# Layer 0's activations normalised before the projection, and ScalarE instead of VectorE evicting its tiles

## Chip, cores and metric

One core of a Trainium2 chip runs one inference step. The metric is the device time of that core in microseconds, the median of several executions; lower is better.

## What is computed

A decoder of two layers works on 512 prompt rows and 8 sample rows of width 1024. Layer 0 is a Mamba-2 state-space mixer, layer 1 a gated position mixer; each is followed by a squared-ReLU MLP. The part that matters here, from the reference:

```python
def rmsnorm(x, g):
    xf = x.astype(jnp.float32)
    r = lax.rsqrt(jnp.mean(xf * xf, axis=-1, keepdims=True) + RMS_EPS)
    return (xf * r * g.astype(jnp.float32)).astype(x.dtype)
...
    proj = h @ w_in                       # h = rmsnorm(x): 1024 -> z, x/B/C, dt
    ...
    conv = conv_b + xbc_ext[:, 0:l] * conv_w[0]
    for k in range(1, SSD_CONV_K):
        conv = conv + xbc_ext[:, k:k + l] * conv_w[k]
    xbc_act = jax.nn.silu(conv)
    ...
    dt = jax.nn.softplus(dt_raw + dt_bias)
    y, h_final = ssd_scan(xs, dt, A, Bm, Cm, h0)
    y = (y + xs * d_skip) * jax.nn.silu(z)
```

## The kernel before

All activations lie transposed, features on the 128 partitions and the 520 rows along the free axis (`xT`, 8 tiles). Every product is done in three passes for accuracy: weights and activations are split into a high and a low part (`w_hi`, `w_lo`, `h_hi`, `h_lo`), so a **unit** of 128 output features is 8 tiles x 3 products x 2 halves of some 260 rows, 48 matmuls (L500), into two PSUM banks. Units come in **pairs** of 256 weight columns. A pair is loaded by SyncE, its high part is written by ScalarE (`split_w`, L897), its low part by VectorE (L1492), each when the pair before last has been multiplied. Two slots of banks (0, 1 and 2, 3) alternate, so a unit waits until the unit before last has been evicted.

The RMS norm of x is not applied to x but to the results: x is only multiplied by the gain, the projection is computed from that, and each evicted tile is multiplied by `rstd`, one value per row, repeated on all partitions. That needs the squares of `xT` (ScalarE, L916), their sum over tiles (GpSimd, L1342), the sum over partitions by a matmul (`stats`, L543), a root (ScalarE, L929) and a reciprocal of 520 values (VectorE, L1515).

Layer 0 does first the pair of dt (32 columns, padded to 128), then for each of 8 groups six units: C and B (0, 1), the two x tiles (2, 3) and two z tiles (4, 5). A **window** `g` on each engine is the work of group g's scan together with units 4 and 5 of g and units 0 to 3 of the next group; every engine has this order written out by hand. The out-projection stands in two parts, after windows 4 and 7. VectorE's part of a window is its queue of:

- `evac_unit`: raw convolution tile out of PSUM times `rstd` (L1561 for the samples' columns, L1563 for the prompt's), or z times `rstd` (L1498), which ScalarE then puts through silu in place (`silu_z`, L1003);
- `conv`: the taps 1 to 3 (L1575), after ScalarE has written tap 0 (`tap0`, L992) from the evicted tile;
- `decayed` (L1606), `y_norm` (L1584, L1587), `sample` (product L1618, reduction L1622), the multiply by decay `xdte` (L1724), `states` and `combine` (ends with L1675).

GpSimd's part is a sum of squares (`y_sum`, L1356), loading of the sample states, two at a time, and four times per window their update: decay L1410, outer product L1420, addition L1424 twice each; then the stores, and once per window two low parts (L1366). It begins, beside the sum, with a small transfer (L1400) of B and C, which ScalarE evicts (L1106). `sample` n on VectorE waits for update n on GpSimd, the sum waits for two squares by ScalarE (L1024), and these wait for `combine`. TensorE's small transposes of the raw tiles (`raw_tr`, L583) wait for their eviction.

At the start SyncE loads x in four chunks of 128 rows, ScalarE issues some 17 small transfers, and TensorE transposes x (L554) and the convolution's parameters (L568). After the dt unit a chain of small operations on ScalarE and VectorE gives the decays (L1144 to L1157, L1749 to L1765), TensorE transposes them (L720) and VectorE copies them (L1768).

## Time and profile before

| | |
|---|---|
| median of 3 executions | 1663.0 us (1662.29 to 1666.39) |
| span of the profiled execution | 1663.9 us |
| TensorE busy | 1560.4 us, 94% |
| VectorE busy | 942.6 us, 57% |
| ScalarE busy | 593.2 us, 36% |
| GpSimd busy | 389.1 us, 23% |
| granted TensorE clock, mean | 0.976 |
| HBM over the span | 103 GB/s |

The span runs from the first to the last instruction of the core. The profile gives no other time for that execution: its span lies 0.9 us above the median, and what lies around it is within the spread of the executions. In 40 slices of the span TensorE is at nine tenths or more from the 17th on; its gaps are in the first 600 us.

### The profile page before, as it was taken

The numbers are of one execution on the slowest core, as the hardware profiler recorded it, in microseconds if no ns is written. First come the engines' busy times: TensorE is split into PE (matmuls) and PEld (weight loads), VectorE is DVE, ScalarE is ACT, GpSimd is POOL, SyncE is SP. The second block draws the span as 40 slices with busy tenths as digits, with TensorE's granted clock in tenths as the row PEclk, the third lists the DMA queues.
The fourth block names the chain that finished last, engine by engine and source line by source line (L and its number), as shares of the span: only waits on it lengthen the run. The fifth ranks groups of instructions, "written<-read, shape, count | busy, mean of one in ns | idle before, by whom it ended". The sixth has DMA issues, their size and how long they took to land.

```text
span 1663.9 us, 30150 instructions
## 1 busy us (share of the span) xinstructions
PE 1560.4 (94%) x12617; PEld 1538.8 (92%) x12617; DVE 942.6 (57%) x1101; ACT 593.2 (36%) x755; POOL 389.1 (23%) x437
## 2 busy tenths in 40 slices
PE   5898988899887999999999999999999999999996
PEld 5888888899887899999999999999999999999996
DVE  4688898863988774343435453464445435344353
ACT  3746644625465342221212343432234212122221
POOL 3076676631777420000000122100001000000001
PEclk9999999899998999999999999999999999999998
DMA  5445354433444323233232333222232332323221
GB/s 162 110 138 155 122 159 144 133 125 112 132 151 131 118 77 102 76 102 98 79 101 77 102 102 102 77 79 77 80 99 77 102 100 79 103 77 102 77 77 52
DMA packets 158919, 173.34 MB, mean 104 GB/s; under 512 B 13912, under 2 KB 146896, under 8 KB 158784
## 3 DMA queue, kind: packets, MB, share of 16 engines
q1 hardware_dynamic: 137032, 131.30, 25.8%
q0 software_dynamic: 9472, 26.50, 4.9%
q10 hardware_dynamic: 12288, 13.71, 2.9%
q8 instruction: 97, 1.59, 0.4%
q14 instruction: 30, 0.25, 0.0%
HBM read 159.53 MB, written 12.21 MB: 103 GB/s over the span
## 4 chain that ended last, share of the span: by engine, by line
PE 64%; DVE 1%; ACT 1%; issue 0%; POOL 0%; ACTq 0%; DVEq 0%
PE ps L500 61%; PE ps L842 1%; PE ps L520 0%; PE ps L810 0%; ACT w_hi L897 0%; PE ps L757 0%; DVE h_lo L1509 0%; PE ps L543 0%; DVE xT L1805 0%; DVE w_lo L1492 0%; POOL ssum L1356 0%; ACT arena L1300 0%; PE ps L834 0%; POOL arena L1424 0%; DVE work L1498 0%
## 5 line engine op out<-in xcount | busy, mean ns | idle before, releaser
L500 PE MATMUL ps<-h_hi,w_hi 128*128 128x260 f32 (+2 forms) x2320 | 485.5, 291 | 12.2 <-issue 4.9
L500 PE MATMUL ps<-h_lo,w_hi 128*128 128x260 f32 (+2 forms) x2320 | 474.9, 287 | 0.1
L500 PE MATMUL ps<-h_hi,w_lo 128*128 128x260 f32 (+2 forms) x2320 | 474.8, 287 | 0.0
L1492 DVE TENSOR_TENSOR w_lo<-w,w_hi 128x2048 fp32r<-128x2048 f32 (+2 forms) x122 | 278.7, 2285 | 185.6 <-ACT w_hi L897 185.6
L500 PEld LDWEIGHTS ps<-h_hi,w_hi 128*128 128x128 f32 x2320 | 368.6, 193 | 14.7 <-issue 12.4
L500 PEld LDWEIGHTS ps<-h_lo,w_hi 128*128 128x128 f32 x2320 | 366.4, 193 | 0.4 <-issue 0.4
L500 PEld LDWEIGHTS ps<-h_hi,w_lo 128*128 128x128 f32 x2320 | 365.9, 192 | 0.0
L897 ACT ACTIVATE w_hi<-w 128x2048 fp32r<-128x2048 f32 (+2 forms) x122 | 229.7, 1884 | 313.2 <-PE ps L500 313.2
L500 PE MATMUL ps<-a_hi,w_hi 128*128 128x260 f32 x1504 | 305.5, 284 | 7.9 <-DVE a_lo L1599 5.5
L500 PE MATMUL ps<-a_hi,w_lo 128*128 128x260 f32 x1504 | 304.4, 284 | 0.0
L500 PE MATMUL ps<-a_lo,w_hi 128*128 128x260 f32 x1504 | 304.1, 284 | 0.0
L1342 POOL TENSOR_TENSOR ssum<-ssum,sq 128x520 f32<-128x520 f32 x35 | 48.3, 1380 | 903.8 <-ACT sq L916 902.8
L500 PEld LDWEIGHTS ps<-a_hi,w_hi 128*128 128x128 f32 x1504 | 233.3, 190 | 8.7 <-issue 5.8
L500 PEld LDWEIGHTS ps<-a_hi,w_lo 128*128 128x128 f32 x1504 | 233.3, 190 | 0.0
L500 PEld LDWEIGHTS ps<-a_lo,w_hi 128*128 128x128 f32 x1504 | 232.9, 190 | 0.0
L1504 DVE TENSOR_TENSOR xT<-ps,xT 128x520 f32<-128x520 f32 x96 | 66.8, 697 | 249.1 <-PE ps L500 249.1
L1498 DVE TENSOR_TENSOR work<-ps,rstd 128x520 f32<-128x520 f32 x96 | 66.9, 697 | 167.9 <-PE ps L500 167.6
L1233 ACT ACTIVATE a_hi<-work 128x520 fp32r<-128x520 f32 x64 | 40.9, 638 | 286.4 <-DVE work L1837 286.4
L1575 DVE SCALAR_TENSOR_TENSOR arena<-arena,convf 128x544 f32<-128x544 f32 x96 | 88.8, 925 | 11.6 <-ACT arena L992 9.1
L992 ACT ACTIVATE arena<-arena,convf 128x544 f32<-128x544 f32 x32 | 26.8, 841 | 120.2 <-DVE arena L1563 120.1
L1420 POOL TENSOR_TENSOR arena<-arena 128x256 f32<-128x256 f32 x64 | 57.8, 902 | 17.1 <-DMA arena<-scr_bc 11.4
L1424 POOL TENSOR_TENSOR arena<-arena 128x256 f32<-128x256 f32 x64 | 57.1, 891 | 5.0
(196 smaller groups left out, 1354.0 us busy)
## 6 DMA issues: line engine op xcount, KB each, us to landing
w<-in_mlp_w_up SPq DMA_DIRECT2D x32, 1024.0 KB, 5.7
w<-in_mlp_w_down SPq DMA_DIRECT2D x32, 1024.0 KB, 5.2
w<-in_ssd_w_in SPq DMA_DIRECT2D x16, 1024.0 KB, 6.5
w<-in_cm_w_in SPq DMA_DIRECT2D x16, 1024.0 KB, 5.7
w<-in_ssd_w_in SPq DMA_DIRECT2D x16, 512.0 KB, 5.6
arena<-in_state_ssm POOLq DMA_DIRECT2D x64, 128.0 KB, 3.4
arena<-scr_a ACTq DMA_DIRECT2D x16, 512.0 KB, 3.7
arena<-scr_bc POOLq DMA_DIRECT2D x32, 256.0 KB, 3.7
```

The costliest lines, as they stand in the source:

```text
L500: mm = pe.matmul(ps[:, 2 * slot + b, 0:tn], w[:, pair.slot, k, col:col + P], x[:, k, t0:t0 + tn], start=(k == 0 and n == 0), stop=(k == ti ...
L842: mm = pe.matmul(ps[:, 4 + j % 2, c * CH:(c + 1) * CH], vtok[:, c, j * P:(j + 1) * P], wmixT[:, j // 2, :], start=True, stop=True)
L897: nc.scalar.activation(w_hi[:, pair.slot, k, w], w32[:, pair.slot, k, w], ACT.Copy)\
L992: nc.scalar.activation(act[:, g % 2, t, :], raw[:, t % 2, 0:CONV_N], ACT.Identity, bias=convf[:, k, 4:5], scale=convf[:, k, 0:1]).then_inc ...
L1233: nc.scalar.activation(a_hi[:, j, :], work[:, half, :], ACT.Copy).then_inc(a_hi_done, 1)
L1342: nc.gpsimd.tensor_tensor(ssum[:, :], ssum[:, :], sq[:, m % 2, :], ALU.add).then_inc(ssum_added, 1)
L1420: nc.gpsimd.tensor_tensor(outer[:, :, :], bcs[:, n % 2, :, 0:N], xdts[:, i, b0:b0 + 2].unsqueeze(2).broadcast_to([P, 2, N]), ALU.mult)\
L1424: nc.gpsimd.tensor_tensor(state[:, 2 * i:2 * i + 2, :], state[:, 2 * i:2 * i + 2, :], outer[:, :, :], ALU.add).then_inc(state_added, 1)
L1492: nc.vector.tensor_tensor(w_lo[:, pair.slot, k, w], w32[:, pair.slot, k, w], w_hi[:, pair.slot, k, w].bitcast(F32), ALU.subtract).then_inc ...
L1498: nc.vector.tensor_tensor(halves(dst), psum_tok(1 - half)[0:n], halves(rstd[0:n, :]), ALU.mult)\
L1504: nc.vector.tensor_tensor(halves(xT[:, m, :]), psum_tok(1 - half), halves(xT[:, m, :]), ALU.add)\
L1575: nc.vector.scalar_tensor_tensor(out=act[:, g % 2, t, :], in0=raw[:, t % 2, tap:tap + CONV_N], scalar=convf[:, k, tap:tap + 1], in1=act[:, ...
```

## The change

For layer 0 alone, the norm is applied to x itself. ScalarE sums the squares of each chunk's rows as the chunk lands (`x_square`: one instruction per chunk, with a per-row accumulator, into `r_x`), takes the roots, VectorE the reciprocals, and ScalarE writes the scaled rows `xn`. TensorE transposes x as before (now 512 prompt and 8 sample columns into one pair of banks, `rows_up`) and then `xn` the same way. `h_hi` and `h_lo` are made from the transposed `xn` in PSUM. The squares, sums, `stats`, root and reciprocal of `xT` for layer 0 are gone, and tiles of layer 0 need no factor when they are evicted: ScalarE copies the raw tiles out of PSUM just before its `tap0` (`raw_evac`), and `silu_z` reads z from PSUM and evicts it by that. VectorE adds dt's bias straight out of PSUM. The dt pair is split as 32 columns, and the padding is cleared in `w_hi` and `w_lo`. Counters of the other norms move down by one.

```diff
@@ SyncE
-                sp.dma_start(xtok[:, c, :], x_prompt[0, c * P:(c + 1) * P, :]).then_inc(x_landed, 16)
-            sp.wait_ge(w_cleared, 1)
+                sp.dma_start(xtok[:, c, :], x_prompt[0, c * P:(c + 1) * P, :]).then_inc(x_landed[c], 16)
@@ TensorE
+            def rows_up(m, rows, row, done):
+
+                bank = 4 + 2 * (m % 2)
+                for c in range(NC):
+                    pe.transpose(ps[:, bank, c * P:(c + 1) * P], rows[:, c, m * P:(m + 1) * P], ident[:, :])
+                pe.transpose(ps[:, bank + 1, 0:NS], row[:, m * P:(m + 1) * P], ident[0:NS, 0:NS]).then_inc(done, 1)
...
+            pe.wait_ge(xn_done, NC + 1)
+            for m in range(KT):
+                pe.wait_ge(x_ready, min(7 + m, KT))
+                if due(m - 1):
+                    pe.wait_ge(h_lo_ready, m - 1)
+                rows_up(m, xn, xn_row, xnt_done)
...
             unit(Pair(J_DT), 1, h_hi, h_lo, k_ready=h_ready(0))
-            stats(0)
@@ ScalarE
+            act_e.wait_ge(xs_landed, 16)
+            x_square(xs_row[:, :], junk_lo[0:NS, 0:D], r_x[0:NS, NC:NC + 1])
+            for c in range(NC):
+                act_e.wait_ge(x_landed[c], 16)
+                x_square(xtok[:, c, :], junk_hi[:, c * D:(c + 1) * D], r_x[:, c:c + 1])
...
+            split_w(Pair(J_DT))
+            act_e.wait_ge(xrec_done, 2)
+            nc.scalar.activation(xn_row[:, :], xs_row[:, :], ACT.Copy, scale=r_x[0:NS, NC:NC + 1]).then_inc(xn_done, 1)
+            for c in range(NC):
+                nc.scalar.activation(xn[:, c, :], xtok[:, c, :], ACT.Copy, scale=r_x[:, c:c + 1]).then_inc(xn_done, 1)
             act_e.wait_ge(feat_ready, 1)
             for m in range(KT):
-                make_h(0, m, G_MIX, x_prologue, 0)
-            split_w(Pair(J_DT))
-            split_w(Pair(1))
-            act_e.wait_ge(const_ready, 2)
-            root(0)
+                act_e.wait_ge(xnt_done, m + 1)
+                nc.scalar.activation(h_hi[:, m, :], psum_flat(4 + 2 * (m % 2)), ACT.Copy, scale=feat[:, G_MIX + m:G_MIX + m + 1])\
+                  .then_inc(h_hi_ready, 1)
+                if m == 3:
+                    split_w(Pair(1))
             split_w(Pair(2))
...
+            def raw_evac(g, t):
...
+                act_e.wait_ge(unit_done, pair.unit(half, 1))
...
+                nc.scalar.activation(raw[:, half, S0 + TAPS - 1:RAW:TAPS], ps[:, bank + 1, 256:256 + NS], ACT.Copy)\
+                  .then_inc(new_evac, 1)
+                nc.scalar.activation(halves(raw[:, half, TAPS - 1:TAPS - 1 + TP]), ps[:, bank:bank + 2, 0:256], ACT.Copy)\
+                  .then_inc(evac_done, 1)
+
             def tap0(g, t):
 
+                raw_evac(g, t)
...
-                nc.scalar.activation(zs[:, i, :], zs[:, i, :], ACT.Silu).then_inc(z_silu_done, 1)
+                nc.scalar.activation(halves(zs[:, i, :]), psum_tok(1 - i), ACT.Silu).then_inc(evac_done, 1)
...
                 silu(g, 3)
+                silu_z(g, 0)
                 cst(g)
...
                 state_evac(g - 1)
-                silu_z(g, 0)
                 exp_m(g, 0)
@@ VectorE
-            inv_rms(0)
...
-                nc.vector.tensor_tensor(halves(raw[:, t % 2, TAPS - 1:TAPS - 1 + TP]), ps[:, 2 * slot:2 * slot + 2, 0:256],
-                                        halves(rstd[:, 0:TP]), ALU.mult).then_inc(evac_done, 1)
...
-                evac_unit(g, 4)
...
-                evac_unit(g, 5)
...
-                evac_unit(nxt, 0)
...
-            evac_scaled(Pair(J_DT), 1, dt_v[:, :], HEADS)
-            dve.wait_ge(evac_done, 1)
             dve.wait_ge(par_landed, 48)
             dve.wait_ge(const_ready, 4)
-            nc.vector.tensor_scalar(dt_v[:, :], dt_v[:, :], dt_par[:, 0:1], None, ALU.add).then_inc(dt_vec_done, 1)
+            dve.wait_ge(unit_done, 1)
+            nc.vector.tensor_scalar(halves(dt_v[:, :]), psum_tok(0)[0:HEADS], dt_par[:, 0:1], None, ALU.add)\
+              .then_inc(evac_done, 1)
```

Three places in the order of instructions. `arena` holds nearly all the temporary tiles, `ps` is PSUM, and `w` the loaded weights.

ScalarE before the dt unit and behind it: before, the splits of the dt pair and pair 1, the root, the split of pair 2, dt's parameters and the start of its chain.

```order
L897 ACTIVATE w_hi<-w 128x8x128
L897 ACTIVATE w_hi<-w 128x2048
L929 ACT_TABLE_LOAD
L929 ACTIVATE ssum<-ps,eps 128x520
L897 ACTIVATE w_hi<-w 128x2048
L1142 DMA arena<-in_ssd_dt_bias 32x1
L1142 DMA arena<-in_ssd_a_log 32x1
L1142 DMA arena<-in_ssd_d 32x1
L1144 ACT_TABLE_LOAD
L1144 ACTIVATE arena<-arena 32x1
L1146 ACTIVATE arena<-arena 32x520
```

The same place after; `h_hi` now comes out of PSUM, and nothing but the split of pair 2 stands between the last `h_hi` and dt's parameters.

```order
L995 ACTIVATE h_hi<-ps,feat 128x520 x4
L914 ACTIVATE w_hi<-w 128x2048
L995 ACTIVATE h_hi<-ps,feat 128x520 x4
L914 ACTIVATE w_hi<-w 128x2048
L1201 DMA arena<-in_ssd_dt_bias 32x1
L1201 DMA arena<-in_ssd_a_log 32x1
L1201 DMA arena<-in_ssd_d 32x1
L1203 ACT_TABLE_LOAD
L1203 ACTIVATE arena<-arena 32x1
L1205 ACTIVATE arena<-arena 32x520
```

The root and its table are gone from here, the splits have moved into the stretch ahead, and pair 2's split is still ahead of dt's parameters.

ScalarE at the end of dt's chain: before, the two transfers to scratch, two fills of the sample columns, `tap0` of the first two tiles, the loads from scratch, silu.

```order
L1160 DMA scr_a<-arena 32x512
L1161 DMA scr_s<-arena 32x24
L978 ACTIVATE arena<-convf 128x8x3 x2
L992 ACTIVATE arena<-arena,convf 128x544 x2
L1170 DMA dtf<-scr_s 64x16x20 x2
L1172 DMA cdec<-scr_s 128x32x4
L998 ACT_TABLE_LOAD
L998 ACTIVATE arena<-arena 128x544 x2
```

The same place after: the raw evictions (L1031, L1033) stand in front of each `tap0`.

```order
L1219 DMA scr_a<-arena 32x512
L1220 DMA scr_s<-arena 32x24
L1013 ACTIVATE arena<-convf 128x8x3 x2
L1031 ACTIVATE arena<-ps 128x8
L1033 ACTIVATE arena<-ps 128x512
L1048 ACTIVATE arena<-arena,convf 128x544
L1031 ACTIVATE arena<-ps 128x8
L1033 ACTIVATE arena<-ps 128x512
L1048 ACTIVATE arena<-arena,convf 128x544
L1229 DMA dtf<-scr_s 64x16x20 x2
L1231 DMA cdec<-scr_s 128x32x4
L1054 ACT_TABLE_LOAD
```

So the eviction of the very first convolution unit has moved behind the whole chain of dt on ScalarE.

VectorE in the middle of window 0: before, the eviction of group 1's unit 0, the decay multiplies, `y_diag`, conv, the eviction of unit 1, `sample`.

```order
L1561 TENSOR_TENSOR arena<-ps,rstd 128x8
L1563 TENSOR_TENSOR arena<-ps,rstd 128x512
L1606 TENSOR_TENSOR arena<-arena 128x512 x2
L1630 SCALAR_TENSOR_TENSOR work<-arena,dtf,ps 128x512
L1575 SCALAR_TENSOR_TENSOR arena<-arena,convf 128x544 x3
L1561 TENSOR_TENSOR arena<-ps,rstd 128x8
L1563 TENSOR_TENSOR arena<-ps,rstd 128x512
L1618 TENSOR_TENSOR sq<-arena 128x512
L1622 TENSOR_REDUCE arena<-sq 128x2x2
L1492 TENSOR_TENSOR w_lo<-w,w_hi 128x2048
```

The same place after.

```order
L1649 TENSOR_TENSOR arena<-arena 128x512 x2
L1671 SCALAR_TENSOR_TENSOR work<-arena,dtf,ps 128x512
L1618 SCALAR_TENSOR_TENSOR arena<-arena,convf 128x544 x3
L1659 TENSOR_TENSOR sq<-arena 128x512
L1663 TENSOR_REDUCE arena<-sq 128x2x2
L1551 TENSOR_TENSOR w_lo<-w,w_hi 128x2048
```

The evictions (L1561, L1563) are gone and the rest keeps its order.

## Rows read from the trace of the kernel before

**Rows 1.** Page, part 1: TensorE's busy time, share of the span, instructions.

```profile
PE 1560.4 (94%) x12617; PEld 1538.8 (92%) x12617; DVE 942.6 (57%) x1101; ACT 593.2 (36%) x755; POOL 389.1 (23%) x437
```

**Rows 2.** Waits of TensorE, 80 to 540 us: total, times, longest.

```profile
PE ps L583 <- DVE arena L1563: 19.0, 6, 3.3
PE ps L689 <- DVE arena L1724: 11.9, 7, 3.4
```

**Rows 3.** View by windows, window 3: length; busy PE, PEld, DVE, ACT, POOL; clock, DMA.

```profile
243.57:300.12 56.55, 48.28 (x368) 46.51 (x368) 49.82 (x63) 32.21 (x54) 38.64 (x44) 0.93 0.47 143
```

**Rows 4.** Timeline of POOL (GpSimd), window 3: start, duration, instruction, idle before.

```profile
243.57 2.61 POOL L1356 TENSOR_TENSOR ssum<-ssum,sq 128x520 f32<-128x520 f32 x1 [3.06 <-ACT sq L1024]
...
255.68 0.61 POOL L1420 TENSOR_TENSOR arena<-arena 128x256 f32<-128x256 f32 x1 [1.46 <-DMA arena<-scr_bc]
...
278.31 1.42 POOL L1420 TENSOR_TENSOR arena<-arena 128x256 f32<-128x256 f32 x1
...
292.75 1.10 POOL L1424 TENSOR_TENSOR arena<-arena 128x256 f32<-128x256 f32 x1
...
300.12 2.60 POOL L1356 TENSOR_TENSOR ssum<-ssum,sq 128x520 f32<-128x520 f32 x1 [3.06 <-ACT sq L1024]
```

**Rows 5.** Timeline of DVE (VectorE): end of window 1, then window 3.

```profile
180.99 0.69 DVE L1618 TENSOR_TENSOR sq<-arena 128x512 f32<-128x512 f32 x1 [0.63 <-POOL arena L1424]
...
244.93 0.69 DVE L1498 TENSOR_TENSOR arena<-ps,rstd 128x520 f32<-128x520 f32 x1
...
262.04 0.67 DVE L1563 TENSOR_TENSOR arena<-ps,rstd 128x512 f32<-128x512 f32 x1
...
269.75 1.23 DVE L1618 TENSOR_TENSOR sq<-arena 128x512 f32<-128x512 f32 x1
...
272.65 2.29 DVE L1492 TENSOR_TENSOR w_lo<-w,w_hi 128x2048 fp32r<-128x2048 f32 x1 [0.95 <-ACT w_hi L897]
...
277.19 2.07 DVE L1724 TENSOR_TENSOR arena<-arena,tokS 128x1024 f32<-128x1024 f32 x1
...
294.36 0.68 DVE L1618 TENSOR_TENSOR sq<-arena 128x512 f32<-128x512 f32 x1
...
298.66 0.70 DVE L1675 TENSOR_TENSOR work<-work,arena 128x520 f32<-128x520 f32 x1
```

**Rows 6.** Timeline of PE (TensorE), start-up.

```profile
18.75 1.11 PE L554 MATMUL ps<-ident,arena 128*128 128x128 f32 x4 [0.15 <-DVE xT L1521]
...
23.21 3.61 PE L568 MATMUL ps<-ident,arena 29*128 29x29 f32 x32
...
30.93 0.77 PE L500 MATMUL ps<-h_hi,w_hi 128*128 128x260 f32 x2 [4.10 <-DVE w_lo L1492]
...
38.72 0.40 PE L500 MATMUL ps<-h_hi,w_lo 128*128 128x260 f32 x2
...
58.01 0.94 PE L720 MATMUL ps<-ident,arena 32*128 32x32 f32 x12
...
69.86 0.66 PE L500 MATMUL ps<-h_hi,w_hi 128*128 128x260 f32 x2 [4.71 <-issue]
```

**Rows 7.** Timeline of ACT (ScalarE; ACTq its transfers), start-up, window 0, window 3.

```profile
8.93 0.70 ACTq L951 DMA_DIRECT2D out<-in_state_conv  x1
...
15.94 0.62 ACT L916 ACTIVATE ssum<-xT 128x520 f32<-128x520 f32 x1
...
40.23 0.34 ACTq L1142 DMA_DIRECT2D arena<-in_ssd_dt_bias  x1
...
41.96 1.91 ACT L897 ACTIVATE w_hi<-w 128x2048 fp32r<-128x2048 f32 x1
...
43.89 1.28 ACT L1144 ACT_TABLE_LOAD   x1
...
46.77 0.64 ACT L1146 ACTIVATE arena<-arena 32x520 f32<-32x520 f32 x1 [1.39 <-DVE arena L1749]
...
57.23 0.34 ACT L978 ACTIVATE arena<-convf 128x24 f32<-128x24 f32 x2 [0.98 <-ACT arena L1157]
...
94.55 0.57 ACT L1122 ACTIVATE arena<-ps 128x512 f32<-128x512 f32 x1
...
247.18 0.63 ACT L1003 ACTIVATE arena<-arena 128x520 f32<-128x520 f32 x1
```

**Rows 8.** Timeline of DVE, start-up and end of window 0.

```profile
16.06 0.76 DVE L1509 SCALAR_TENSOR_TENSOR h_lo<-xT,feat,h_hi 128x520 fp32r<-128x520 f32 x1 [0.74 <-ACT h_hi L923]
...
52.35 0.17 DVE L1561 TENSOR_TENSOR arena<-ps,rstd 128x8 f32<-128x8 f32 x1 [2.68 <-PE ps L500]
...
124.49 0.69 DVE L1618 TENSOR_TENSOR sq<-arena 128x512 f32<-128x512 f32 x1
```

**Rows 9.** Timeline of POOL, last state of window 0.

```profile
121.61 0.74 POOL L1424 TENSOR_TENSOR arena<-arena 128x256 f32<-128x256 f32 x1
```

214 lines of the change are left out of this document (114 added, 100 removed).

## Prediction

> **What bounds the kernel now.** I read the page's busy shares first, then for whom TensorE waits, then the timelines of VectorE and GpSimd through one window of layer 0, and last the start-up. TensorE is busy 94% of the span [rows 1] and its gaps lie in the first 600 us, so what this change gives or takes lies in the start-up and in the eight windows. There TensorE waits for VectorE: the longest entry, 19.0 us in 6 waits, is the transpose (L583) of a raw tile that VectorE has still to evict (L1563) [rows 2]. This looks like the cost that the change removes.
>
> But a wait is worth only what no other chain holds. Window 3 lasts 56.55 us, from one sum of squares on GpSimd (243.57) to the next (300.12) [rows 4]. VectorE is busy 49.8 us of it, ScalarE 32.2, GpSimd 38.6 [rows 3]; GpSimd's work is one chain with its own transfers in between, and its last state is ready at 293.85 (292.75 + 1.10). VectorE takes it at 294.36 [rows 4, 5]: the slack is 0.5 us. In window 1 VectorE waited 0.63 us for GpSimd (180.99) [rows 5]. From there on the path is fixed: `sample`, `combine` (to 299.36), two squares on ScalarE, GpSimd's next sum. So a window has two nearly equal bounds, VectorE's queue and GpSimd's chain, and the change shortens only the first.
>
> **The change part by part.** *Evictions.* VectorE loses in each window four raw evictions at 0.67 us and two of z at 0.69 (a little less from start to start) [rows 5]: 3.9 us. Two hand-overs from VectorE to ScalarE and back, like the wait of 0.95 at 272.65 [rows 5], go too. But the eviction at 262.04 costs nothing now, since GpSimd holds up the multiply behind it, and the two of z stand where VectorE waits anyhow. Its queue would get 2 to 3 us ahead per window. ScalarE takes the raw tiles over at some 0.6 to 0.8 us each (0.57 for the same size out of PSUM [rows 7], and the samples' small one); with 24 us idle per window [rows 3] this is free. But VectorE would then wait for GpSimd, and the window shrinks by the slack alone: 0.5 us in windows 2, 3, 5 and 6, together -2.0. Against it, silu of z (0.63 [rows 7]) now stands ahead of the B/C eviction that GpSimd's first transfer waits for. GpSimd comes late to that wait except in window 5, where it costs 0.6, and about 0.1 in the others: +1.1. Sum of windows 1 to 7: -0.9.
>
> *GpSimd's own speed.* Its multiply takes 0.61 us alone and 1.42 beside VectorE [rows 4]; VectorE's product takes 0.68 or 1.23 [rows 5]. They hold each other up, and which meets which after the change no row shows. Lower bound: the last operations of a window run free, since VectorE's conv is over by then: -0.8 per window, one such collision. Upper bound: I laid window 3's operations end to end without the evictions; GpSimd's addition then meets the product at 269.75 (+0.55) and the next four operations meet a conv (+0.4): +0.9. I take 0, in the middle, over 6 windows; the bounds are -4.8 and +5.4.
>
> The Trainium skill (SBUF — State Buffer, section Who interferes with whom) says that a VectorE instruction with two SBUF inputs shuts out a GpSimd instruction that reads SBUF, and one with a single SBUF input does not. The evictions have one input in PSUM, so by this rule the harmless operations leave and the harmful ones move closer together: +5.4 by the rule instead of 0, which speaks against the change.
>
> *Start-up.* Now the dt unit starts at 30.93 and ends at 39.12 [rows 6]. After, ScalarE is free at 9.63, when its transfers are issued [rows 7]. Then a table load, 1.28, and five squares of 1024 elements at 1.04 (0.62 for 520 and 1.91 for 2048 [rows 7] give 0.84 ns per element): 16.1. The accumulator's price is unknown; between nothing and 0.2 each I take nothing. Second table 1.28, two roots and the reciprocals 0.7: 18.1. Five scalings at 1.04, behind the reciprocals: 23.6. Meanwhile TensorE transposes x from about 11.2 (8 sets of 1.11 and a small one, held up once while VectorE waits for the roots) and the parameters, 3.61 [rows 6], to 25.0. Then x a second time, through two buffers: for two tiles 1.25 on TensorE, 0.7 on ScalarE, 0.76 on VectorE [rows 8] and the hand-overs, 2.9; for eight 11.6; of pair 1's splits in this loop (1.9 and 2.3) some 2.1 shows. The dt unit starts at 38.7, +7.8, and ends at 46.9: it needs its 8.2 us again, as its first pairs of matmuls run at the 1.2 GHz level after a stretch of transposes (0.77 against 0.40 at the end [rows 6]).
>
> On the new table load, the Trainium skill (ScalarE: Activation LUTs, section What ACT_TABLE_LOAD costs) adds a drain of some 1.4 us, 2.66 in all; the row shows 1.28, with the next instruction of ScalarE right behind. By the page the start would be 1.4 us later still; the row stands.
>
> *Behind the dt unit.* ScalarE meets the split of pair 2 first, which waits for the dt unit, and dt's three parameter loads stand behind it: issued from 40.23 now [rows 7], from 47.0 to 48.3 after. They had landed by 43.89, at most 2.4 us after the last issue; between 0 and 2.4 I take 1.9, near the upper end as nothing landed at once: 50.2. From the table load at 43.89 to the first fill at 57.23 it was 13.3 us, less the waits of 1.39 (dt evicted behind the reciprocal) [rows 7] and 2.68 (VectorE at an eviction) [rows 8]: 9.3. So the fills come at 59.5 and the eviction of the first convolution unit, behind them, at 60.3. The third unit needs those banks and could start at 58.4: TensorE waits 1.9 and ends it at 66 to 68 (the upper if its clock drops once more), where it was 58.01 [rows 6]. From there to the first z unit it was 11.85 (69.86) [rows 6]; 10.9 now, as the first conv is done: 77.9, +8.0. All of window 0, with GpSimd's first B/C load, is queued behind.
>
> *Window 0.* VectorE took its last state at 124.49 [rows 8], GpSimd had it at 122.35 [rows 9]: here the VectorE side binds and the change helps by some 1.6 (hand-overs, and the eviction behind the last unit). That gives 130.9, +6.4; GpSimd, moved by 6.5, would be done at 128.9. Bounds: +3 (parameters land at once, no drop of the clock, a tighter loop) and +9 (dear accumulators and hand-overs).
>
> **Sum.** +6.4 - 0.9 + 0 = +5.5. The out-projection after window 4 starts behind that window's `combine` and passes the shift on; behind window 7 nothing is changed. The sum is made against the span, 1663.9, which lies 0.9 above the median; on the median 1663.0 it gives 1668.5, say 1669. A measurement of this kernel tells 0.3%, 5 us, from no change.
>
> **Rivals.** *The windows follow VectorE's queue*, and the change is faster. For it: 19.0 us of TensorE's waits and 3.9 us of VectorE's work per window leave. Against it: the slack of 0.5. It needs GpSimd's chain to shorten by fewer collisions: by 0.9 per window to break even, by 1.6 to show. At 1.6 (twice what the multiply at 278.31 loses) it gives 7 x 1.6 - 6.4, 1658; at VectorE's 2.6 it gives 1651. Chance 0.16. *The start-up is absorbed*: window 0 takes back all but 2 us and the change does nothing in the end, 1660 to 1666. For it: VectorE and ScalarE have many short waits there. Against it: TensorE's order keeps dt's transposes behind the third unit. 0.18. *GpSimd is hit harder*: +0.9 in six windows and +8 at the start, 1676; for it the collisions in the rows, against it that VectorE ends its window earlier. 0.14. *My forecast*: 0.52, 1664 to 1674, 0.32 of it above 1668. So slower is 0.32 + 0.14 = 0.46, same 0.20 + 0.18 = 0.38, faster 0.16. The range, 1657 to 1677, takes in the bounds of the two unknowns and leaves out the outer halves of the first and third rival.
>
> **What would show it.** The dt unit starts at 37 to 40; the third convolution unit waits for ScalarE at 58 to 60; the first z unit starts near 78. The waits of L583 are gone, and TensorE waits instead for the multiply L1724 (5 us per window; now 11.9 in 7 waits [rows 2]), which is VectorE's next late step after 277.19 [rows 5]. VectorE waits 1 to 3 us per window for GpSimd's last state, and the period of windows 1 to 3 stays at 56 to 57. If it falls to 55 or less, I misread the bound, and the kernel is faster; if the dt unit starts before 35, the start-up is wrong.

## The result, and the profile after

The change makes the kernel slower: 1679.8 us (median of 4 runs, 1678.5 to 1682.0) against 1663.3 (4 runs), ratio 1.0092 with a 95% interval of 1.0079 to 1.0106. That is +16.5 us where I had forecast +5.5 and a range up to 1677: the direction was right, the size was three times too small, and the time lies outside the range.

The profiled execution has a span of 1680.3 us. Its busy times (first part of the page; compare [rows 1]) have hardly moved: no engine has become the bound by its work.

```profile
span 1680.3 us, 30210 instructions
PE 1571.3 (94%) x12653; PEld 1545.7 (92%) x12653; DVE 909.1 (54%) x1020; ACT 618.4 (37%) x827; POOL 374.0 (22%) x431
```

Whom TensorE waits for between 95 and 560 us (compare [rows 2]; the view of waits, with total, number and longest):

```profile
PE ps L706 <- DVE arena L1765: 30.6, 7, 5.8
PE ps L636 <- DVE work L1716: 21.6, 6, 5.0
PE ps L682 <- DVE arena L1649: 7.1, 6, 2.3
```

and from the same view, VectorE's wait for GpSimd:

```profile
DVE sq L1659 <- POOL arena L1483: 28.5, 7, 5.7
```

The transpose's wait for an evicted raw tile, 19.0 us before, is gone. In its place TensorE waits for the decayed `xdt` (the multiply L1765, L1724 before), 4.4 us a window, as the prediction said, and for `combine` (L1716), 21.6 us where it was 8.7, which it did not say. VectorE itself now waits for GpSimd's last sample state, 4.1 us a window and up to 5.7, where the prediction said 1 to 3. What the prediction missed altogether is the length of the windows. These rows are GpSimd's sums, one per window, whose distance is the window's period (compare [rows 4]):

```profile
136.12 2.61 POOL L1415 TENSOR_TENSOR ssum<-ssum,sq 128x520 f32<-128x520 f32 x1 [2.60 <-ACT sq L1083]
194.90 2.61 POOL L1415 TENSOR_TENSOR ssum<-ssum,sq 128x520 f32<-128x520 f32 x1 [2.60 <-ACT sq L1083]
253.99 2.60 POOL L1415 TENSOR_TENSOR ssum<-ssum,sq 128x520 f32<-128x520 f32 x1 [2.60 <-ACT sq L1083]
312.19 2.62 POOL L1415 TENSOR_TENSOR ssum<-ssum,sq 128x520 f32<-128x520 f32 x1 [2.60 <-ACT sq L1083]
```

58.8, 59.1 and 58.2 us, where the three periods before were 56.5, 56.8 and 56.55. Three numbers cut the span into parts that all kernels below share: the start of the first such sum ("start"), from it to the last sum ("windows", 1 to 7 with the out-projection in between), and the rest ("tail"). Before: 130.3, 437.2, 1096.5. After: 136.1, 450.6, 1093.5. The start gives +5.8, the windows +13.5, the tail -2.9.

Over all seven windows the view by windows gives, before and then after (length; busy PE, PEld, DVE, ACT, POOL; clock, DMA share, GB/s):

```profile
130.27:567.43 437.16, 383.30 (x2934) 370.06 (x2932) 347.13 (x433) 223.05 (x356) 273.06 (x304) 0.94 0.44 135
```

```profile
136.12:586.76 450.64, 386.49 (x2940) 371.85 (x2939) 325.06 (x371) 237.87 (x404) 264.86 (x305) 0.92 0.45 131
```

GpSimd was busy 8.2 us less, not more, and idle 21.7 us more: the +13.5 lie in its waits. TensorE's granted clock went from 0.94 to 0.92 with them; it goes back to 0.94 when the waits do (0.92 in evict_alone, 0.94 in evict_behind below), and TensorE's busy time grew by 3.2 us only.

**Where a window's 2.3 us come from.** (58.8 against 56.5 in window 1, 59.1 against 56.8 in window 2.) GpSimd makes four updates of sample states per window, and loads the states for the third and the fourth only behind the update ahead of it. Here are the loads for the third update of window 2, the decay that waits for them, and SyncE's weight load, first after and then before (timelines of GpSimd and of SyncE's queue; the last bracket is the idle time and what ended it):

```profile
225.03 1.42 POOL L1441 DMA_DIRECT2D arena<-in_state_ssm  x2
232.58 1.63 POOL L1469 TENSOR_TENSOR arena<-arena,dtf 128x512 f32<-128x512 f32 x1 [6.13 <-DMA arena<-in_state_ssm]
...
225.59 0.37 SPq L413 DMA_DIRECT2D w<-in_ssd_w_in  x1
```

```profile
216.15 1.42 POOL L1382 DMA_DIRECT2D arena<-in_state_ssm  x2
220.23 1.35 POOL L1410 TENSOR_TENSOR arena<-arena,dtf 128x512 f32<-128x512 f32 x1 [2.65 <-DMA arena<-in_state_ssm]
...
218.42 0.37 SPq L402 DMA_DIRECT2D w<-in_ssd_w_in  x1
```

Before, the 1 MB weight load is issued 2.3 us behind the first of the two state loads, in every one of windows 1 to 6. VectorE's split of the weights releases it, and VectorE, 3.9 us of evictions lighter, now comes to that split earlier against GpSimd: the weight load is issued 0.6 us behind the first state load, between the two. The decay waits 6.1 us for its states in place of 2.7. What the DMA queues moved between the state load's issue and the decay (queue: packets, MB, busy share of 16 engines), after and then before:

```profile
q1 hardware_dynamic: 1036, 1.05, 44.2%
q0 software_dynamic: 224, 0.66, 43.8%
q10 hardware_dynamic: 52, 0.21, 7.6%
```

```profile
q0 software_dynamic: 224, 0.66, 51.2%
q1 hardware_dynamic: 67, 0.07, 11.0%
```

GpSimd's queue moved the same 0.66 MB, but shared the engines with the whole weight load, half and half. The Trainium skill (DMA: Bandwidth & Descriptors, section Queues, rings and completion order) says that a DMA engine takes turns between its queues, one packet at a time; the equal shares agree. The wait is 5.9 to 6.1 us in windows 1, 2, 4, 5 and 6 and 3.3 in window 3, where the weight load comes 2.1 us behind the second state load. Summed over the six windows it went from 16.0 to 33.2 us. (q10 is a load by ScalarE, which does not stand in the stretch of before; the first experiment below tells it from the weight load.)

The start-up, beside [rows 6] (TensorE's timeline: the dt unit's first matmul, the third convolution unit, the first z unit):

```profile
38.75 0.80 PE L510 MATMUL ps<-h_hi,w_hi 128*128 128x260 f32 x2
...
58.30 0.48 PE L510 MATMUL ps<-h_hi,w_hi 128*128 128x256 f32 x2 [0.55 <-ACT arena L1033]
...
75.86 0.51 PE L510 MATMUL ps<-h_hi,w_hi 128*128 128x260 f32 x2 [4.46 <-issue]
```

The dt unit was forecast for 38.7, the third unit to wait from 58.4 to 60.3, the first z unit for 77.9.

### The profile page after: what moved, and what is told of

Read it like the earlier page. It is cut to its first block, busy times and chain, and to the rows that moved or that the text cites. A ratio compares the mean times of both kernels' runs of the same rounds, so it can differ in the third digit from the quotient of the medians.

```text
span 1680.3 us, 30210 instructions
## 1 busy us (share of the span) xinstructions
PE 1571.3 (94%) x12653; PEld 1545.7 (92%) x12653; DVE 909.1 (54%) x1020; ACT 618.4 (37%) x827; POOL 374.0 (22%) x431
## 4 chain that ended last, share of the span: by engine, by line
PE 63%; DVE 1%; ACT 1%; issue 0%; POOL 0%; ACTq 0%; DVEq 0%
PE ps L510 61%; PE ps L859 1%; PE ps L530 1%; PE ps L827 0%; PE ps L774 0%; PE ps L553 0%; DVE w_lo L1551 0%; PE ps L625 0%; POOL ssum L1415 0%; ACT arena L1359 0%; ACT w_hi L914 0%; PE ps L899 0%; PE ps L851 0%; POOL arena L1483 0%; DVE work L1557 0%
## 5 line engine op out<-in xcount | busy, mean ns | idle before, releaser
L1402 POOL TENSOR_TENSOR ssum<-ssum,sq 128x520 f32<-128x520 f32 x28 | 39.1, 1395 | 881.4 <-ACT sq L933 880.6
L1563 DVE TENSOR_TENSOR xT<-ps,xT 128x520 f32<-128x520 f32 x96 | 66.9, 698 | 252.7 <-PE ps L510 252.7
L706 PE MATMUL ps<-arena 128*128 128x256 f32 x64 | 25.2, 562 | 30.6 <-DVE arena L1765 30.6
```

Of the source, the lines that this page charges most:

```text
L706: mm = pe.matmul(ps[:, 6 if c < 2 else 4, (c % 2) * 256:(c % 2) * 256 + 256], Btok[:, c, :], xdt[:, c, :], start=True, stop=True)
L1402: nc.gpsimd.tensor_tensor(ssum[:, :], ssum[:, :], sq[:, m % 2, :], ALU.add).then_inc(ssum_added, 1)
L1563: nc.vector.tensor_tensor(halves(xT[:, m, :]), psum_tok(1 - half), halves(xT[:, m, :]), ALU.add)\
```

## The experiments

All medians stand against runs of the kernel before on the same chip, whose own median was 1664.2 to 1667.8 us, so the ratio is what compares. Start, windows and tail are from the one profiled execution, whose own time stands under "profiled": it can lie several us from the median (z_back 6.0 below it, start_pad 6.2 above, evict_behind 3.6 below, before_pad96 3.8 above), and then the parts say less than the medians. "Third" and "fourth" are GpSimd's waits for the states of these updates in windows 1 to 6.

| run | us | ratio [95%] | profiled | start | windows | tail | third | fourth |
|---|---|---|---|---|---|---|---|---|
| before | | | about 1665.6 | 130.3 | 437.2 | 1096.5 | 2.5-2.8 | 2.4-2.9 |
| after | 1679.8 | 1.0092 [1.0079, 1.0106] | 1682.0 | 136.1 | 450.6 | 1093.5 | 3.3-6.1 | 2.7-3.4 |
| start_alone | 1679.1 | 1.0087 [1.0069, 1.0106] | 1679.1 | 137.1 | 446.0 | 1094.4 | 2.7-3.5 | 2.8-4.5 |
| evict_alone | 1681.3 | 1.0105 [1.0084, 1.0127] | 1680.4 | 132.2 | 450.2 | 1096.3 | 2.8-6.3 | 2.8-4.4 |
| weight_behind | 1674.1 | 1.0053 [1.0037, 1.0069] | 1674.0 | 136.1 | 442.7 | 1093.5 | 2.8-3.1 | 3.0-4.4 |
| z_back | 1682.9 | 1.0109 [1.0089, 1.0129] | 1676.9 | 135.4 | 448.4 | 1091.3 | 5.6-6.1 | 2.7-3.2 |
| evict_behind | 1666.0 | 1.0015 [1.0006, 1.0024] | 1662.5 | 131.7 | 432.1 | 1096.9 | 2.7-3.1 | 2.7-3.0 |
| start_pad | 1681.8 | 1.0101 [1.0082, 1.0120] | 1688.0 | 141.8 | 450.9 | 1093.6 | 3.4-4.7 | 2.8-3.8 |
| before_pad | 1662.6 | 0.9988 [0.9977, 0.9999] | 1661.1 | 129.0 | 438.0 | 1092.3 | 2.6-3.0 | 2.6-2.9 |
| behind_pad | 1679.5 | 1.0097 [1.0080, 1.0114] | 1679.5 | 137.2 | 438.4 | 1102.0 | 2.9-3.1 | 2.6-3.8 |
| start_aligned | 1688.1 | 1.0122 [1.0099, 1.0146] | 1688.4 | 145.4 | 444.9 | 1096.5 | 2.8-3.6 | 2.8-4.3 |
| behind_aligned | 1686.3 | 1.0114 [1.0089, 1.0139] | 1684.1 | 145.2 | 440.9 | 1096.3 | 2.8-3.2 | 2.8-3.8 |
| before_pad80 | 1670.9 | 1.0015 [0.9999, 1.0030] | 1672.4 | 130.5 | 446.7 | 1093.5 | 2.7-3.0 | 2.9-4.4 |
| before_pad96 | 1669.0 | 1.0029 [1.0016, 1.0041] | 1672.8 | 131.1 | 446.8 | 1093.2 | 2.2-2.9 | 2.8-4.6 |
| start_spread | 1677.9 | 1.0087 [1.0072, 1.0102] | 1676.2 | 136.0 | 441.5 | 1097.0 | 2.8-3.3 | 2.7-3.8 |
| behind_spread | 1674.5 | 1.0066 [1.0052, 1.0080] | 1672.2 | 136.0 | 436.7 | 1097.7 | 2.8-3.1 | 2.9-3.7 |
| after_sp_states | 1652.8 | 0.9929 [0.9912, 0.9946] | 1652.4 | 134.1 | 422.4 | 1094.0 | none | none |
| before_sp_states | 1658.8 | 0.9943 [0.9925, 0.9961] | 1658.8 | 130.8 | 430.2 | 1096.1 | 3.7-4.4 | 0.8-1.9 |

(For the kernel before, the time of the profiled execution is worked out: its span, 1663.9, and the 1.7 us or so by which the time exceeds the span in all the others. It lies some 2 us above that kernel's median.)

**The repair of the weight load** (cause A), in the changed kernel:

```diff
@@ SyncE, stage: for the weight load that the third split of windows 1 to 6 releases
+                if isinstance(pair.loop, int) and pair.s in third:
+                    sp.wait_ge(hst_landed[0], 32 * (2 * third[pair.s] + 2))
```

> The changed kernel with one more wait on SyncE's queue: in windows 1 to 6 the 1 MB weight load that the window's third weight split releases is issued only when the sample states of that window's third update have landed. Theory A (in the changed kernel this weight load is issued between the two halves of GpSimd's state load, the two share the DMA engines, and GpSimd's decay waits 5.9 to 6.1 us for its states where it waited 2.7 before): the wait before the third decay is back at 2.6 to 3.5 us in every window, windows 1, 2, 4, 5 and 6 are each 1.8 to 2.6 us shorter, and the kernel takes 1668 to 1671. Theory B (GpSimd and VectorE collide more, the late states are only a symptom): the states come earlier, the updates behind them are slower by as much, 1676 or more. Theory C (ScalarE's own loads for the decay factors or GpSimd's descriptor writing make the states late): the wait stays over 5.5 us, 1679 to 1681.

The third wait is back at 2.8 to 3.1 us in every window, and the ratio falls from 1.0092 to 1.0053, some 6 us; the 1668 to 1671 of theory A are missed. Theory C is out. Of B a part is true: GpSimd was busy 270.6 us over the windows, 5.8 more than in the changed kernel, so over a third of the 15.2 us that the third waits gave back went into slower instructions. The windows keep 5.5 us more than before, and in windows 4 to 6 the fourth wait has become 3.9 to 4.4 us.

**The two parts of the change, each alone.** First the new start with VectorE evicting as before, in plain copies:

```diff
-                raw_evac(g, t)                       (ScalarE, ahead of tap0; silu_z back on SBUF)
+                evac_unit(nxt, 0) ... evac_unit(nxt, 3), evac_unit(g, 4), evac_unit(g, 5)   (VectorE, old places)
```

> The start-up of the changed kernel (activations normalised ahead of the projection) with the evictions given back to VectorE at their old places, as plain copies; ScalarE takes silu from SBUF as before. Theory A: only the start-up's term is left, the first z unit starts near 75.9, windows 1 to 6 last 56 to 57 us as before, and the kernel takes 1668 to 1671 (before plus 5.5 to 7). Theory B (the longer windows come from the changed start, by the phase of GpSimd's chain against the others): the windows stay at 58 to 59 and it takes 1677 or more. Theory C (the plain copies are so much cheaper for VectorE that the windows gain): below 1667.

Theory A is wrong here: without any change in the evictions the windows take 446.0 us. No third wait is above 3.5 us; the weight load stands 2.3 us behind the first state load, as before. The fourth waits are long, 3.9, 4.5 and 4.4 us in windows 3, 4 and 6. So there was a second cause.

Then the evictions alone, on the kernel before. VectorE's multiplication by `rstd` went with its evictions, so this kernel leaves out that factor for the raw tiles and z:

```diff
+                raw_evac(g, t)                       (ScalarE, ahead of tap0)
-                evac_unit(...)                       (VectorE, all of the first layer)
```

> The evictions alone: the start-up of the kernel before (row sums by squares, root and reciprocal beside the first units), with ScalarE evicting the convolution tiles and z as in the changed kernel. The factor 1/rms of each token is left out of the convolution tiles and of z of the first layer (dt keeps it), since it would need VectorE. Theory A: the longer windows belong to this part: third decay waits 5.8 to 6.1 us for its states in most windows, periods 58 to 59, 1672 to 1676. Theory B (the two parts matter only together): periods 56 to 57, 1661 to 1666.

Theory A holds: the third load is hit in windows 1, 2, 4, 5 and 6, and the windows take 450.2 us. The loss, larger than the 1672 to 1676 expected, is not a matter of both parts together: each part alone costs about as much as the two.

> The changed kernel with ScalarE's eviction of z's first tile (silu, 0.65 us) put back behind the eviction of B and C rows and of the states, its place in the kernel before. GpSimd's window then starts its updates about 0.6 us earlier against the weight split. Theory A: the state load of the third update is then issued whole ahead of the weight load (29.5 and 30.2 against 30.6 after the window's sum), so that the collision goes in most windows at once: wait 2.7 to 3.5 us, 1667 to 1672. Theory B (a term in proportion: only the 0.65 us comes back in each of 7 windows): 1675 to 1677. Theory C (nothing comes back): 1679 to 1681.

(`silu_z(g, 0)` moved back behind `state_evac(g - 1)`.) In the medians nothing comes back, theory C: GpSimd's and VectorE's later work move together by it, and the weight load, at 29.8 to 30.7 us of a window, still comes between the state loads, at 29.2 to 30.1 and 0.7 later.

**The weight load without the new start.** This is the clean test of cause A, since evict_alone has no other change near the windows. The edit is that of weight_behind on evict_alone, and it leaves out the same factor.

> The evictions alone (start-up of the kernel before, TensorE's program as long as there, 22632 instructions; the token factor 1/rms left out of the first layer's convolution tiles and z) with the third weight load of windows 1 to 6 held until the third update's states have landed. The evictions alone took 1681.3, windows 1 to 7 450.2 us, third waits 4.8 to 6.3 us in windows 1, 2, 4, 5 and 6. Cause A (the weight load that the lighter VectorE lets SyncE issue between the two state loads): third waits 2.6 to 3.2 us, windows 438 to 443 us, 1668 to 1673. If the evictions slow the windows in another way: windows over 446, 1677 or more.

The third update's loads and decay and the weight load of window 2, in evict_alone and then in evict_behind (timelines of GpSimd and SyncE's queue):

```profile
220.39 1.43 POOL L1406 DMA_DIRECT2D arena<-in_state_ssm  x2
227.55 1.19 POOL L1434 TENSOR_TENSOR arena<-arena,dtf 128x512 f32<-128x512 f32 x1 [5.74 <-DMA arena<-in_state_ssm]
...
220.95 0.37 SPq L401 DMA_DIRECT2D w<-in_ssd_w_in  x1
```

```profile
217.59 1.43 POOL L1410 DMA_DIRECT2D arena<-in_state_ssm  x2
221.81 1.03 POOL L1438 TENSOR_TENSOR arena<-arena,dtf 128x512 f32<-128x512 f32 x1 [2.79 <-DMA arena<-in_state_ssm]
...
221.80 0.37 SPq L405 DMA_DIRECT2D w<-in_ssd_w_in  x1
```

One wait on SyncE's queue takes the kernel from 1.0105 to 1.0015, 15 us, and the windows from 450.2 to 432.1. Cause A is shown. The profiled execution has windows 5.1 us shorter than before, beyond the 438 to 443 expected, but that does not show that the evictions pay: it was the fastest of twelve, the median is 1.8 us above that of the kernel before (ratio 1.0015, interval clear of 1), and 4.7 of the 5.1 us stand in GpSimd's waits for its transfer of B and C (22.8 us against 27.5), which landed 1.6 to 6.6 us behind its issue in the windows of all these kernels, for no reason that I found. Over the whole study the third wait goes with the distance of the weight load: 4.8 to 6.3 us in the 16 windows where it was issued 0.6 or 0.8 us behind the first state load, 3.6 at most where it came 2.3 us or more behind and no code packet (see below) fell in between.

**The code packets** (cause D). In start_alone TensorE's code arrives in packets of 0.02 MB on a queue of its own (q8), 12 to 25 us apart in the windows, 19 in the mean, with some 250 weight loads and matmuls of TensorE from one to the next; where one fell into the fourth state load, the load was slow. Waits on a semaphore that is already there shift these packets without any change of work (two of them make one instruction in the page's count):

```diff
             pe.wait_ge(ident_ready, 4)
+            for _ in range(2 * N):
+                pe.wait_ge(ident_ready, 4)
```

with N = 128 on start_alone, 48 on the kernel before, 64 on weight_behind.

> The start-up alone (new start, evictions on VectorE), with 256 more waits on a semaphore that is already there at the head of TensorE's program, which the program packs into 128 instructions; no work is changed, and TensorE is idle there until x lands. In the trace of the start-up alone, TensorE's code arrives in packets of 0.02 MB, one every 17 to 20 us, and in windows 3, 4 and 6 one falls between the issue and the landing of GpSimd's state load for the fourth update, whose wait is then 3.9 to 4.5 us against 2.4 to 2.9 in the kernel before, where these packets fall behind the load. Theory D (a code packet on one of the 16 DMA engines holds up the state load, and what is TensorE's instruction count decides where it falls): 128 instructions move the packets by half a period, some 9 us earlier in the work, to 33 to 36 us and 52 to 55 us of each window; the fourth wait is 2.4 to 3.2 us in all windows, the windows are 1 to 1.5 us shorter, and the kernel takes 1670 to 1674 where the start-up alone took 1679. Theory E (the packets are a coincidence): 1677 to 1681.

The fourth wait falls to 2.8 to 3.1 us in five of six windows, as D says, but the packets land at 32 to 35 us, in the third load, whose wait rises to 3.4 to 4.7: the hit moved with the packet. I had reckoned 33 to 36 us, behind that load; it lasts until 35. The total says nothing: the 128 instructions held TensorE's first matmul until 15.7 us (10.0 in start_alone), and the start is 4.7 us later.

> The kernel before, with 96 more waits (48 instructions) at the head of TensorE's program and nothing else. Theory D: TensorE's code packets, which came 44.7 to 48.9 us behind the window's sum, just behind the landing of the fourth update's states (45 us), come about 3.5 us earlier, into that load (41 to 45 us): the fourth wait grows from 2.4 to 2.9 us to 3.3 to 4.5 us in most windows, and the kernel takes 1667 to 1673 with no change in its work. Theory E: 1662 to 1666.

The packets moved to 45 to 46 us only (51 in window 4), still at the end of the load or behind it; no test.

> The changed kernel with the third weight load held behind the state load (1674 in its own run) and 64 more instructions of waits at TensorE's head. Its code packets fell at 41.3 to 44.8 us of each window, in windows 4 to 6 within the fourth update's load (waits 3.9 to 4.4 us). Theory D: they fall some 4.7 us earlier, at 36 to 40 us, between the two loads: fourth wait 2.6 to 3.2 us, 1668 to 1671. Theory E: 1673 to 1676.

The windows are repaired, 438.4 us, but the tail grew by 8.5, which both theories lacked (last section).

Then with the shift counted: the new start adds 80 instructions to TensorE's program, and N = 176 completes a packet's 256.

> The start-up alone with 176 instructions of waits ahead of TensorE's work. TensorE's program of the start-up alone has 80 instructions more than that of the kernel before (22712 against 22632, all ahead of the windows); with 176 it has 256 more, and one code packet carries 0.02 MB, some 256 instructions of 64 bytes. So the packets should fall at the places of the kernel before (7, 27 and 45 to 48 us of a window). Theory D: third wait 2.5 to 3.2 us, fourth 2.4 to 3.2 us in all windows, windows 1 to 7 together 436 to 440 us as before (437.2; the start-up alone took 446.0), and the kernel takes 1667 to 1672, the start-up's own term. Theory E (the new start slows the windows in another way): windows 444 to 448, 1676 to 1681.

> The changed kernel with both repairs: the third weight load behind the state load, and TensorE's code aligned as in the kernel before (176 instructions of waits at its head). If the weight load and the code packets are the two causes of the longer windows, windows 1 to 7 take 437 to 441 us (450.6 in the changed kernel, 437.2 before, 442.7 with the first repair alone) and the kernel 1667 to 1672; what is left is the start-up. If only the first counts: 1673 to 1676. The stretch behind the windows took 1091 to 1102 us in the runs so far and may blur this; the windows are the test.

The 176 instructions take longer than TensorE's idle time at the head (its first matmul comes at 20.9 us in both): the start is 8 to 9 us later, and the totals say nothing. In the windows, both repairs together give 440.9 us, as D and A expect; the start alone 444.9, not the 436 to 440 expected, with windows 3 and 4 still long.

> The kernel before with 80 instructions of waits at TensorE's head, the shift that the new start-up gives its code, and no other change. Theory D: packets at 41 to 45 us of most windows as in the start-up alone, fourth wait 3.3 to 4.5 us in at least three windows, windows 1 to 7 together 441 to 447 us (437.2 before), 1667 to 1673. Theory E, or packets that fall just behind the load as they did with 48 instructions: 437 to 439 us, 1661 to 1666.

This is the clearest view of D: the kernel before, its work untouched, with the 80 instructions of the new start as waits. The fourth update of window 2, before and then with the 80 (GpSimd's timeline), and the queues in that stretch of the latter:

```profile
228.20 1.42 POOL L1382 DMA_DIRECT2D arena<-in_state_ssm  x2
232.47 1.03 POOL L1410 TENSOR_TENSOR arena<-arena,dtf 128x512 f32<-128x512 f32 x1 [2.85 <-DMA arena<-in_state_ssm]
```

```profile
228.13 1.42 POOL L1384 DMA_DIRECT2D arena<-in_state_ssm  x2
233.94 1.03 POOL L1412 TENSOR_TENSOR arena<-arena,dtf 128x512 f32<-128x512 f32 x1 [4.39 <-DMA arena<-in_state_ssm]
```

```profile
q0 software_dynamic: 224, 0.66, 38.8%
q8 instruction: 1, 0.02, 1.0%
q14 instruction: 1, 0.01, 0.3%
```

The same load, nothing else on the queues but one packet on q8: 1.5 us longer. (A q14 packet alone, as before had there, did no harm here.) The fourth waits are 4.4, 3.4, 4.4, 4.1 and 4.4 us in windows 2 to 6, the windows 446.7 us. The median, 3 us above the kernel before, is not outside the noise of that chip; so it was tried once more, a little further:

> The kernel before with 96 instructions of waits at TensorE's head, 16 more than in the run with 80, in which the code packets fell into the fourth update's load in windows 2, 4, 5 and 6 (waits 4.1 to 4.4 us) and the windows took 446.7 us. Cause D: packets another 1 us earlier, 40 to 44 us, fourth waits of 3.3 to 4.5 us in at least three windows, windows 441 to 448 us, and 3 to 9 us above the kernel before on the same chip. If the run with 80 was chance: windows 437 to 439 us, within 3 us of the kernel before.

1.0029, the interval clear of 1: +4.8 us, windows 446.8. In this profile three of the waits are long (3.5, 4.1, 4.6); windows 3 and 4 are long through their first updates instead. Both profiled executions were slower than their medians, so the +9.5 us of windows, against 2.5 and 4.8 of the ratios, are the upper end.

All kernels together settle what a packet does. In the 16 in which GpSimd issues the loads there are 96 fourth loads in windows 1 to 6. Into 34 of them a q8 packet fell: waits 2.6 to 4.6 us, median 3.6. In the 62 others they are 2.4 to 3.8, median 2.9. All 15 waits above 3.8 us have the packet; but 19 loads with one were not that slow. With the two padded kernels before, this shows the packet as the cause of the longest fourth waits; it does not act each time. That the place of TensorE's code moves this kernel's time is shown; that each long window is a packet in a state load is not.

The Trainium skill (Runtime: NRT & Kernel Launch, section Instruction fetch mechanics) says that an engine's code is fetched in blocks of 256 instructions by a DMA queue of its own, and that crossing a block's end is mostly hidden. The packets' size and rhythm agree. For a state load that was under way it is not hidden, as the waits show.

Last, the 176 spread so that they cost nothing at the start:

```diff
+            64 at the head as above, and ahead of each of the 16 groups of transpositions:
+                for _ in range(14):
+                    pe.wait_ge(ident_ready, 4)
```

> The start-up alone with the same 176 instructions of waits, 64 at TensorE's head and 7 ahead of each of the 16 groups of transpositions, where it idles; in the run with all of them at the head, they made the start 8.3 us longer and hid what the windows gave. Cause D (code packets): start of the windows' count within 3 us of the start-up alone (137.1), windows 438 to 444 us (446.0 in the start-up alone), 1671 to 1676 against its 1679. If the code's place does not matter: 1678 to 1683.

> The changed kernel with both repairs, the third weight load behind the state load and the 176 instructions spread in the same way. Causes A and D: windows 438 to 442 us, and 1668 to 1674, the start-up's 6 us above the kernel before and little more. If only A counts: 1674 to 1678 (the first repair alone took 1674.1).

In the profiles the windows come down as expected, 446.0 to 441.5 and 442.7 to 436.7, with both repairs as long as before. The medians don't follow: 1.0087 against 1.0087, and 1.0066 against 1.0053, which is where the expectation put "only A counts". The profiled executions were the fastest of five and of six, and the tail takes back 2.6 and 4.2 us. So this repair of the code's place gave the kernel no time, and what D costs the changed kernel itself is not shown; its fourth waits were 2.7 to 3.4 us.

**GpSimd's loads given to SyncE.** If the chain of update, issue, landing and update is the bound, taking load and issue out of it must pay more than any repair:

```diff
@@ SyncE, stage, around the weight load that the third split of window g releases
+                    load_states(4 * g + 2)           (waits for smul_done and sstored as on GpSimd)
                 sp.dma_start(w32[...], src)
+                    load_states(4 * g + 3), load_states(4 * g + 4), load_states(4 * g + 5)
@@ GpSimd
-                load_states(...)
```

> The changed kernel with the loads of the sample states issued by SyncE (hardware queue) as soon as their buffer is free, the third update's ahead of the third weight load, in place of GpSimd after its update. Theory A and D share that GpSimd's chain is the bound of windows 1 to 7 and that in it each update waits for a load issued only behind the update before. If so, 1.4 us of issuing and 2.7 to 6 us of waiting leave the chain at the third and the fourth update of each window, VectorE no longer waits for the last state (2 to 5.7 us a window, 32.8 in all), the windows follow VectorE's own work at 52 to 55 us, and the kernel takes 1643 to 1658, below the kernel before. Rival (another chain holds the windows close behind, TensorE's waits for VectorE's products): under 10 us of gain, 1670 to 1676. Rival (the loads of SyncE hold its weight loads back): slower than 1680.

1652.8 us, ratio 0.9929: 27 us faster than the changed kernel and 12 than the kernel before. The third state load is now issued ahead of the weight load, so the 27 contain the 6 of cause A. GpSimd and SyncE's queue in window 2:

```profile
218.11 1.37 POOL L1483 TENSOR_TENSOR arena<-arena,dtf 128x512 f32<-128x512 f32 x1
221.99 1.31 POOL L1493 TENSOR_TENSOR arena<-arena 128x256 f32<-128x256 f32 x1 [2.51 <-DMA arena<-scr_bc]
...
215.18 0.88 SPq L417 DMA_DIRECT2D arena<-in_state_ssm  x2
218.65 0.37 SPq L436 DMA_DIRECT2D w<-in_ssd_w_in  x1
```

and the busy times of window 2 (PE, PEld, DVE, ACT, POOL), here and in the changed kernel, behind the window and its length (then clock, DMA share and GB/s):

```profile
188.71:243.32 54.61, 48.63 (x374) 46.56 (x374) 45.89 (x53) 34.73 (x62) 34.56 (x37) 0.94 0.53 148
```

```profile
194.90:253.99 59.09, 49.03 (x374) 46.84 (x374) 45.14 (x53) 34.68 (x62) 38.27 (x45) 0.93 0.49 137
```

The decay waits for nothing, a state load lands in 2.4 us in place of 3.8 (medians), VectorE's 28.5 us of waits for GpSimd's last state are down to one of 2.4, and the window falls from 59.1 to 54.6 with nearly the same work on TensorE, VectorE and ScalarE. The bound is confirmed.

The Trainium skill (DMA: Bandwidth & Descriptors, section Issuing engine by pattern) gives plain loads to SyncE; the run agrees.

> The kernel before with the state loads issued by SyncE, as in the same edit of the changed kernel (1652.8). It asks what the evictions on ScalarE are worth once GpSimd's chain is not the bound. If windows then follow VectorE's work, this one, with 5 to 6 us more of it in each window, takes longer in windows 1 to 7 than the 422.4 us of the changed kernel with this edit, and gives back about the 6 us that its start-up is shorter: windows 428 to 434, 1652 to 1660. If VectorE's evictions are still hidden: windows 422 to 426, 1645 to 1650.

The windows take 430.2 us against 422.4, as expected of VectorE's added work: once GpSimd's chain is out of the way, the evictions on ScalarE are worth 7.7 us in the windows of these two profiles (both at their medians), of which the later start takes 3.3. The ratios, 0.9943 and 0.9929, differ by less than their intervals, so in the kernel's time the gain is not shown. Giving the loads to SyncE alone made the kernel before some 9.5 us faster.

## Why the prediction was right in direction and wrong in size

*The bound.* Right. GpSimd's chain holds the windows: VectorE's lighter queue turned into 28.5 us of waiting for GpSimd, L583's waits went, those for `xdt` came. Taking the loads out of that chain gave 27 us in the changed kernel and 9.5 in the one before.

*The start-up.* Right in the main: the dt unit at 38.75 (38.7 forecast), the third unit waiting for ScalarE at 58.3, though 0.6 us and not 1.9, the first z unit at 75.9 (77.9). The 2 us too many are the wait for dt's parameters: ScalarE's chain of dt began at 48.2, right behind the split of pair 2, where I had it wait until 50.2, and the fills came at 57.3, not 59.5.

*Window 0.* It moved by 5.8 us where I had 6.4, and that is luck. I had VectorE as its bound, at 130.9, and GpSimd done at 128.9. GpSimd was done at 130.3 and VectorE waited 2.1 us for it: GpSimd's chain held this window too, and the 1.6 us that I gave the lighter VectorE did not come.

*The windows.* This is the step that failed: -0.9 for windows 1 to 7, and 0 for "GpSimd's own speed" with bounds of -4.8 and +5.4. They gave +13.5. I asked only which engine GpSimd's instructions would meet, and left the transfers between them as long as they were, with a wait of 2.7 us for the third states: a term put at nothing without a reason. GpSimd's instructions did not slow down; they took 8.2 us less. What changed is the landing of the state loads: the third waits alone grew from 16.0 to 33.2 us. (The silu of z ahead of the B/C eviction cost what I had forecast: GpSimd's wait for that eviction grew by 1.1 us, from 0.9 to 2.0.) The growth is cause A and moves with VectorE: repaired, it gives back 7.9 us of windows and some 6 of the total in the changed kernel, 18 and 15 in the evictions alone. D moves with the length of TensorE's program, and showed itself in the start-up alone and when A was repaired: the 80 or 96 instructions alone cost the kernel before 2.5 (interval down to 0) and 4.8 us.

*The rule on shared ports*, by which the evictions' going would cost +5.4: not borne out. With the load repaired, GpSimd was busy 273.6 us over the windows of evict_behind and 270.6 in weight_behind, against 273.1 before.

*The rivals.* That of an absorbed start-up is out (+5.8 stands at the end of window 0). "GpSimd is hit harder" had the right sign and place but not the mechanism: it meant collisions with VectorE. The rival that the windows follow VectorE needs what after_sp_states does.

*The tail* was taken as unchanged and gave -2.9 (last section).

What stays open: the parts do not add. Each half of the change costs what the whole does (1.0087 and 1.0105 against 1.0092), and with both repairs (behind_spread) the median is still 10 us above its own runs of before, of which the start explains 6. Window 3 is long (58.2 us) without a late third load: GpSimd's wait for its transfer of B and C was 5.45 us there against 3.93 before, and what delays that transfer I did not find.

## What to carry to other kernels

A wait that ends with a transfer is not a fixed price: before moving work off an engine, list what that engine's instructions release on the queues, and look which transfers of the bounding chain are in flight at that moment. If the bound is a chain of update, load and update, first take the load out of the chain (another queue, issued as soon as the buffer is free): here that was worth 9.5 us in the kernel before and 27 in the changed one. Differences under 0.5% came here from the place of TensorE's code alone (0.29% with 96 instructions of waits), so a small gain or loss is best judged beside a run with padding that changes nothing else. And the parts read from one profiled execution are no better than that execution: look first how far its time lies from the median.

## What the runs showed of the hardware

- A code packet of TensorE (0.02 MB; in before_pad80 1.0% of 16 DMA engines over 5.8 us, some 0.9 us of one engine) delays a state load of 2 x 128 KB by 1 to 1.8 us (fourth wait 3.9 to 4.6 us against 2.4 to 2.9), but not each time: in weight_behind a packet fell into the fourth load in windows 1 and 3 too, with waits of 3.0 us.
- The tail, whose code is the same in all runs but for its place, takes 1096.1 to 1097.7 us in the eight kernels whose TensorE program is as long as before or 256 instructions longer, and 1091.3 to 1094.4 in the eight with 48, 80 or 96 more. One wait of TensorE for split weights shows in the former and not in the latter (view of waits behind 640 us, first row, before and after):

```profile
PE ps L500 <- ACT w_hi L897: 2.7, 1, 2.7
```

```profile
PE ps L774 <- DVE arena L1908: 1.5, 1, 1.5
```

  With 144 more (behind_pad) it took 1102.0, with this wait and one of 2.2 us for nothing that the profile shows; with 208 more (start_pad) 1093.6. The code packets tell the two kinds apart: 97 or 98 in the nine kernels with the long tail, 88 or 89 in the nine others. The row of the page, before and after:

```profile
q8 instruction: 97, 1.59, 0.4%
```

```profile
q8 instruction: 88, 1.44, 0.4%
```

  The tail has two loops of two passes, one in each MLP. In the short tails q8 rests twice, for 105 to 111 us in which TensorE does some 1800 weight loads and matmuls, so one pass of each loop needs no new code; in the long ones it rests once, and three packets come within some 5 us in place of the other rest (1453.8 to 1458.6 us in the kernel before), where the wait for split weights also falls (it ends at 1458.4). That the one makes the other is argued from this coincidence, which behind_pad has too (789.7 to 795.0 us, waits ending at 794.2 and 797.2).
- A pair of waits for semaphores that are already there, one instruction in the count, costs TensorE 0.11 us: 48 more of them moved its first matmul by 5.2 us (15.74 in start_pad, 20.90 in start_aligned).
- A state load of 128 KB lands 2.4 or 3.0 us after its issue on SyncE's queue (after_sp_states, before_sp_states) and 3.4 or 3.8 on GpSimd's (before, after), in the medians over 64 loads.
